# Two small norms inside the attention stage: their sum of squares on VectorE, and one product with ones instead of three and two

## What is computed

```python
def rmsnorm(x, g):
    xf = x.astype(jnp.float32)
    y = xf * lax.rsqrt(jnp.mean(xf * xf, axis=-1, keepdims=True) + EPS)
    return (y * g.astype(jnp.float32)).astype(x.dtype)
...
def mla_kv(p_kv, kv_norm, w_ukv, cos, sin):
    b, n = p_kv.shape[:2]
    kv_lat, k_rope = p_kv[..., :KV_LORA], p_kv[..., KV_LORA:]
    kv = (rmsnorm(kv_lat, kv_norm) @ w_ukv).reshape(b, n, MLA_HEADS, QK_NOPE + V_DIM)
...
def mla_q(q_lat, q_norm, w_uq, cos, sin):
    b, n = q_lat.shape[:2]
    q = (rmsnorm(q_lat, q_norm) @ w_uq).reshape(b, n, MLA_HEADS, QK_NOPE + QK_ROPE)
```

## Time and profile before

| | us |
|---|---|
| median of 3 runs (2588.94, 2591.19, 2591.07) | 2591.07 |
| the profiled execution | 2596.06 |
| its span | 2594.3 |
| TensorE busy in it | 2537.3 (98%) |
| VectorE busy | 1657.2 (64%) |
| ScalarE busy | 1296.0 (50%) |
| mean granted clock of TensorE | 0.994 |

### The profile page before, as it was taken

The page is one execution under the profiler, slowest core; times in us unless marked ns, Lnnn a source line. Parts: engine busy times, 40 slices in busy tenths (PEclk is TensorE's granted clock), DMA queues, the critical chain, the costliest instruction groups (busy, mean ns, idle before and its releaser), DMA issues.

```text
span 2594.3 us, 44764 instructions
## 1 busy us (share of the span) xinstructions
PE 2537.3 (98%) x18300; PEld 2229.7 (86%) x18300; DVE 1657.2 (64%) x2360; ACT 1296.0 (50%) x2086; POOL 89.0 (3%) x103
## 2 busy tenths in 40 slices
PE   7999999999999999999999999999999999999999
PEld 7999999899899888888876788888888888867999
DVE  6888786787887766364534577355566374645655
ACT  5554664555465566173335467254375273445443
POOL 2001100000100000000030000000000000010000
PEclk9999999999999999999999999999999999999999
DMA  8456767545765646444333345545346454453673
GB/s 240 140 153 195 192 180 213 179 134 160 211 195 164 204 119 175 121 134 133 111 91 114 115 120 166 145 122 143 116 120 173 122 142 125 125 169 99 186 209 110
DMA packets 613411, 393.48 MB, mean 152 GB/s; under 512 B 47304, under 2 KB 608950, under 8 KB 613109
## 3 DMA queue, kind: packets, MB, share of 16 engines
q1 hardware_dynamic: 610164, 383.14, 51.6%
q0 software_dynamic: 2176, 6.58, 1.1%
q10 hardware_dynamic: 896, 1.31, 0.2%
HBM read 389.94 MB, written 1.05 MB: 151 GB/s over the span
## 4 chain that ended last, share of the span: by engine, by line
PE 84%; DVE 7%; ACT 4%; DVEq 2%; issue 1%; POOL 1%; DMA 0%; ACTq 0%
PE acc L1085 11%; PE acc L1086 11%; PE acc L1087 11%; PE scores L1085 6%; PE scores L1086 5%; PE scores L1087 5%; PE scores L1148 3%; PE scores L1149 3%; PE scores L1150 3%; PE acc L1148 3%; PE acc L1149 3%; PE acc L1150 3%; DVEq L2211 2%; ACT prod L1690 1%; ACT raw L1690 1%
## 5 line engine op out<-in xcount | busy, mean ns | idle before, releaser
L1652 ACT ACTIVATE whi<-raw 128x2048 fp32r<-128x2048 f32 (+2 forms) x355 | 570.0, 1611 | 682.0 <-PE scores L1150 191.8
L2229 DVE TENSOR_TENSOR wlo<-raw,whi 128x2048 fp32r<-128x2048 f32 (+2 forms) x297 | 609.6, 2053 | 169.2 <-ACT whi L1652 165.4
L1085 PE MATMUL acc<-h,whi 128*128 128x512 f32 (+1 forms) x988 | 354.6, 359 | 5.0 <-DVE wlo L2229 2.9
L1086 PE MATMUL acc<-h,whi 128*128 128x512 f32 (+1 forms) x988 | 352.2, 356 | 0.0
L1087 PE MATMUL acc<-h,wlo 128*128 128x512 f32 (+1 forms) x988 | 351.8, 356 | 0.0
L1085 PE MATMUL acc<-h_hi,whi 128*128 128x256 f32 x1056 | 301.3, 285 | 3.2 <-DVE wlo L2229 2.9
L1086 PE MATMUL acc<-h_lo,whi 128*128 128x256 f32 x1056 | 295.0, 279 | 0.0
L1087 PE MATMUL acc<-h_hi,wlo 128*128 128x256 f32 x1056 | 294.8, 279 | 0.0
L1085 PE MATMUL scores<-h,whi 128*128 128x512 f32 (+1 forms) x608 | 219.7, 361 | 0.7 <-DVE wlo L2229 0.6
L1086 PE MATMUL scores<-h,whi 128*128 128x512 f32 (+1 forms) x608 | 219.2, 361 | 0.0
L1087 PE MATMUL scores<-h,wlo 128*128 128x512 f32 (+1 forms) x608 | 219.0, 360 | 0.0
(11 more groups left out here) (420 smaller groups left out, 5426.8 us busy)
## 6 DMA issues: line engine op xcount, KB each, us to landing
raw<-in_ffn_w_in_dram SPq DMA_DIRECT2D x176, 512.0 KB, 5.3
raw<-in_w_mod_dram SPq DMA_DIRECT2D x72, 1024.0 KB, 5.1
raw<-in_w_in_dram SPq DMA_DIRECT2D x62, 1024.0 KB, 5.0
raw<-in_w_up_dram SPq DMA_DIRECT2D x88, 512.0 KB, 5.1
raw<-in_ffn_w_out_dram SPq DMA_DIRECT2D x64, 704.0 KB, 4.8
raw<-in_w_down_dram SPq DMA_DIRECT2D x32, 704.0 KB, 4.6
raw<-in_w_out_dram SPq DMA_DIRECT2D x16, 1024.0 KB, 6.2
raw<-in_w_branch_dram SPq DMA_DIRECT2D x16, 512.0 KB, 6.1
```

The source lines that it names most:

```text
L1085: pe.matmul(bank, wh, hi[:, c0 + k, 0:width], start=(k == 0), stop=False)
L1086: pe.matmul(bank, wh, lo[:, c0 + k, 0:width], start=False, stop=False)
L1652: return act.activation(out_, in_, ACT.Copy, **kw)
L2229: dve.tensor_tensor(wlo[:, s % 2, 0:el], raw[:, slot, 0:el], f32(whi[:, s % 2, 0:el]), ALU.subtract).then_inc(s_lo, 1)
```

## The change

The norms made by `norm_rows` get the mark `added`. VectorE adds the squares of the two or three chunks into `rstd` in a new function `add_rows`, and TensorE makes one product of `rstd` with ones when the additions are done. `s_sum` is raised by each addition and by the product, so that it counts as far as before. ScalarE's stream is the same.

```diff
         def norm_rows(src, n, width, gain, hi, lo, c0):
 
-            return dict(chunks=[[(src[:, c, 0:width], 0, width)] for c in range(n)],
+            return dict(chunks=[[(src[:, c, 0:width], 0, width)] for c in range(n)], added=True,
                         width=width, mat=ones, scale=1.0 / (n * P),
...
+                if "added" in spec:
+                    pe.wait_ge(s_sum, n("sum", len(spec["chunks"]) - 1))
+                    n("sq", len(spec["chunks"]))
+                    pe.wait_ge(s_flat, n("norm"))
+                    pe.wait_ge(s_modout, n("mod"))
+                    pe.matmul(stat[:, 0:spec["width"]], spec["mat"], rstd[:, 0:spec["width"]], start=True, stop=True)\
                       .then_inc(s_sum, 1)
                     n("sum", 1)
                     n("norm", 1)
+                    return
...
+            def add_rows(spec):
+
+                w_ = spec["width"]
+                even, odd = (sq[:, (n("chunk") + c) % 2, 0:w_] for c in range(2))
+                dve.wait_ge(s_sq, n("sq") + 2)
+                dve.tensor_tensor(rstd[:, 0:w_], even, odd, ALU.add).then_inc(s_sum, 1)
+                if len(spec["chunks"]) == 3:
+                    dve.wait_ge(s_sq, n("sq") + 3)
+                    settle()
+                    dve.tensor_tensor(rstd[:, 0:w_], rstd[:, 0:w_], even, ALU.add).then_inc(s_sum, 1)
...
-                scale_norm(norm_rows(qr, 3, T, ("q_norm_2", l), h2_hi, h2_lo, 4))
+                q_norm = norm_rows(qr, 3, T, ("q_norm_2", l), h2_hi, h2_lo, 4)
+                add_rows(q_norm)
+                scale_norm(q_norm)
                 rest_next(nm + "kr", 0, None)
                 kv_norm = norm_rows(kvr, 2, 512, ("kv_norm_2", l), h2_hi, h2_lo, 2)
+                add_rows(kv_norm)
                 flatten(kv_norm)
```

More of the change, by code:

```diff
@@ L1013, in norm @@
                     pe.matmul(stat[:, 0:w_], spec["mat"], sq[:, n("sum") % 2, 0:w_], start=False, stop=True)\
+                      .then_inc(s_sum, 1)
+                    n("sum", 1)
+                    n("norm", 1)
+                    return
[5 more added lines that the diff above has]
+                    pe.matmul(stat[:, 0:spec["width"]], spec["mat"], rstd[:, 0:spec["width"]], start=True, stop=True)\
                       .then_inc(s_sum, 1)
```

## The result

The changed kernel takes 2600.35 us (median of 7 runs, 2598.2 to 2601.7), the kernel before 2591.07 us (7 runs, 2588.91 to 2594.83). The ratio is 1.0039, 95% interval 1.0029 to 1.0049: slower by 9.3 us. The forecast was 2601.

A forecast was written before the change was run, and what follows sets the result against it. TensorE, busy 98% of the span, was taken as the bound. Shifts of 3.5 (layer 0) and 2.8 (layer 1) plus 4.0 for the clock gave +10.3 us on 2591.07, say 2601; range 2595.5 to 2606.

The forecast's parts named there:

- q's sum: TensorE's sum for q's norm: two of three products go, additions hidden; gains 1.84 us in layer 0, 1.32 in layer 1.
- kv's wait: TensorE ahead of kv's remaining product: idle until VectorE's late addition, 6.1 us in layer 0, 4.9 in layer 1.
- The shift without the clock: Fourier products behind kv's sum start later, q's gain included: +3.5 us in layer 0, +2.8 in layer 1.
- The clock: TensorE behind the two new idle times: half clock for some us, 2.0 us lost at each, 4.0 together.
- Nothing absorbed: Behind the two stages: later waits swallow none of the loss, 3 us as upper bound.
- The range: Whole kernel's time: from 2595.5 (clock holds, less spread) to 2606 us (3.4 lost at each gap, plus spread).
- The change does what its first half does: Rival: VectorE reaches kv's addition before `kr` ends, so no wait arises; -4.9 us, 2586.2; chance 0.05.

The follow-up runs named there:

- e1: Kernel before with additions and single product for q's norm only, kv's norm unchanged: median 3.2 us below the kernel before, ratio 0.9985.
- e5: Full change with kv's addition on VectorE moved ahead of the 128x1152 weight rest: +7.7 us against the kernel before, ratio 1.0028.
- e4: Full change plus useless repeated Fourier products on TensorE ahead of kv's sum: +4.8 us against the kernel before, ratio 1.0018.
- e3: Full change with kv's addition moved between q's first and second scaled chunk, into the second half of `sq`: -3.8 us against the kernel before, ratio 0.9982.
- e7: The full change run again, unedited: +10.2 us against the kernel before, ratio 1.0037.
- e8: e3 plus ScalarE's two copies of the first Fourier result (`fab`) ahead of q's third rounding: -2.2 us against the kernel before, ratio 0.9992.
- e6: Full change with kv's product on TensorE moved behind the first segment's Fourier products: +3.4 us against the kernel before, ratio 1.0010.

## Why the prediction was right

**q's sum.** Predicted gains 1.84 and 1.32, measured 1.90 and 1.31 (e1; its median is 3.2 us lower, give or take 2.3). The additions were hidden, though the first took 1.77 us and not 0.69 (last section).

**kv's wait.** Predicted idle times 6.1 and 4.9, measured 5.98 and 4.75. The chain shows the steps that the forecast named, in that order; e5 moves one of them, and each idle time shrinks by just that step.

**The shift without the clock.** Predicted +3.5 and +2.8; e4, which keeps the clock up, gives +3.48 and +2.70.

**The clock.** Predicted 2.0 for each idle time, measured 2.62 and 1.71, together 4.3 for the forecast 4.0. The direction was argued from the traces, the size was a choice between nothing and 3.4, and that the sum fits so well is in part luck: one term is 0.6 too small, the other 0.3 too large. The reason given (the slow stretch begins inside the idle time) held in layer 0, where 1.48 us of it lay there, and not in layer 1, where the clock fell after the restart. The two cases that the sizes were read from are also single draws. The pair of waits at the start of the kernel (3.2 to 3.7 us each) stands in all ten profiled executions, and half clock follows it in four of them (before, e3, e5, e7); the wait of 2.16 us near 896 stands in all ten too, with half clock behind it in four (before, the change, e4, e7). The Trainium skill ("TensorE: Matmul & The Clock Gate", Part 1) had the rule that counted here: an idle array falls to half rate. All nine long waits in the two stages agree with it; at the start of the kernel six executions of ten stayed at full clock.

**Nothing absorbed.** Right between the stages, within the spread given above (+0.01). Behind layer 1 the profiled execution of the change is 6.89 us shorter than that of before, which looks like absorption and is for the most part none: the same part is 4.4 to 7.6 us shorter in all nine other profiled executions, e1 and e3 with no loss to absorb among them. The profiled execution of before ran its attention of layer 1 at half clock for some 10 us, that of the change at full clock. The same columns, first before, then the change 12 us later:

```profile
2332.00:2338.00 6.00, 6.00 (x22) 2.66 (x22) 2.00 (x5) 2.88 (x6) 0.00 (x0) 0.50 0.40 136
```
```profile
2344.00:2350.00 6.00, 5.64 (x160) 4.15 (x160) 3.81 (x9) 2.42 (x8) 0.00 (x0) 1.00 0.65 197
```

So one step of the forecast was wrong: I carried the 4.99 us by which the profiled execution of before lay above the median over to the changed kernel (2606.4), and its profiled execution took 2601.17. Those 5 us had been, at least in good part, this half-clock stretch, which the other nine lack there: 10.2 us at half clock, up to 5.1 of them lost. The median did not contain it, and the forecast of the median holds. Why it came in that execution alone stays open.

**The range.** Its ends use 1.9 and 1.8 us as the spread of the shown runs, which spans 2.25 us (2588.94 to 2591.19); with that it would be wider by some 0.4 us at either end.

**A rival's price was wrong.** "The change does what its first half does" was priced at -4.9 us, with 0.86 us for each dropped product of kv. e3 builds that case and gets -3.3 in the stages: kv's dropped product gains 0.1 us in layer 0 and nothing in layer 1. In layer 0 that is ScalarE's order, as e8 shows by taking it away (-2.80 against the priced -2.70). In layer 1 kv's product was never on the path. The chain of the kernel before leaves TensorE at the end of `kr` and comes back only in `uq`; between them it runs over `krope`, the scaling of q, kv's root, the scaling of kv and a weight rest:

```profile
2290.60 0.60 ACT krope L1652
...
2294.66 0.64 DVE root L2271
...
2301.62 1.28 DVE wlo L2229
2302.94 0.38 PE acc L1085
```

From `krope` to that product of `uq` it is 12.34 us before, 12.34 in e1 and 12.35 in e3. So the product saved in e3 only makes TensorE wait longer ahead of `uq`, and both kernels gain q's 1.31.

## What to carry to other kernels

Fewer products on the bound engine are worth nothing if the one that stays waits for an engine whose instruction stands late in its own order; look up what stands ahead of the new producer, not how busy its engine is. Take the half whose additions are covered (q's alone, e1), or move the other's addition ahead of the step that waits (e3): each beats the kernel before by 0.15 to 0.18% and the change by some 0.5%. When a wait opens on TensorE, price it with the clock behind it: here 10.7 us of waits brought about 4.3 us of slow work with them, and useless products in the idle time took that slow work away (e4, +4.8 us instead of +9.3).

## What the runs showed of the hardware

**An addition that took 1.77 us instead of 0.69.** The first addition for q in layer 0, from VectorE's timeline, and GpSimd's timeline at the two places (the last row holds two instructions):

```profile
1334.17 1.77 DVE L2279 TENSOR_TENSOR rstd<-sq 128x512 f32<-128x512 f32 x1
...
1353.56 0.68 DVE L2279 TENSOR_TENSOR rstd<-sq 128x512 f32<-128x512 f32 x1
```
```profile
1331.87 1.30 POOL L983 TENSOR_TENSOR cb<-cb,prt 128x512 f32<-128x512 f32 x1
1333.12 2.27 POOL L983 TENSOR_TENSOR cb<-cb,prt 128x512 f32<-128x512 f32 x1
...
2280.05 2.17 POOL L979 TENSOR_TENSOR prt<-prt 128x256 f32<-128x256 f32 x2
```

GpSimd's second instruction ends at 1335.39, and the addition ends at 1335.94, 0.55 us after that. The two engines take turns: VectorE's rest ahead of the addition (128x1024, 1332.58 to 1334.25) took 1.67 us instead of the 1.22 of layer 1, and GpSimd's second instruction, issued while that rest ran, took 2.27 instead of 1.30. In layer 1 the 256-wide addition took 0.96 instead of 0.42, beside the last row. The addition for kv, with GpSimd idle, took 0.68. The Trainium skill ("SBUF — State Buffer", on the port pair that VectorE and GpSimd share) says that of a VectorE instruction with two SBUF inputs and a GpSimd one that reads SBUF the later waits until the other is through; the times above agree. No run here removed GpSimd's work, so the cause is read, not shown. It cost nothing: behind the two additions VectorE still waited 5.48 us in layer 0 and 8.68 in layer 1 for TensorE's product.

**The clock after shorter waits.** It fell in e5 after 3.48 us idle, and in e8 after 1.85 us. TensorE had been busy without a gap for 6.3 us ahead of that wait (2288.94 to 2295.21), and the clock fell 1.0 us after the restart. In the same stages 1.59 and 1.66 us (e6) and 1.30 us (e4) of idle time left it at full. The wait of 2.16 us near 896 was followed by half clock in four executions of ten. So one trace does not tell what a wait of about 2 us will do to the clock.
